# A decoder layer on one core: single projection groups, scores inside the projection, and four smaller moves of norms, picks and stores

## What is computed

```python
def mix_sample(x, win_k, win_v, sb_k_pool, sb_v_pool, mem_k, mem_v, page_table, mw):
    ...
    qa, ka, va, qb, kb, vb, qm = project_heads(rms_norm(x, g_pre), w_in)
    qa, ka = rope(qa, pos), rope(ka, pos)
    ...
    o_a = combine_by_denominators([dilated_group_gather(qa, k_all, v_all, n_buf, w, d) for w, d in DIL_PATTERNS])
    k_past = sb_k_pool[page_table].reshape(B, n_past, N_HEADS_SB, HEAD_DIM)
    ...
    o_b = sweep_query_blocks(lambda q, qp: stick_breaking_block(q, kb_all, vb_all, qp, sb_bias), qb, pos)
    o_m = memory_attention(qm, mem_k, mem_v)
    y = mixer_output(x, o_a, o_b, o_m, g_out_a, g_out_b, g_out_m, w_out, g_post)
```

## Time and profile before

| | us |
|---|---|
| three runs, median (lowest to highest) | 2225.07 (2220.13 to 2225.96) |
| the profiled execution, its own time | 2226.81 |
| span of its trace | 2225.0 |
| PE busy | 2137.6 (96%) |
| DVE, ACT, POOL busy | 1328.9, 925.1, 414.8 |
| mean granted TensorE clock | 0.986 of full speed |

### The profile page before, as it was taken

The page is one execution under the profiler, slowest core; times in us unless marked ns, Lnnn a source line. Parts: engine busy times, 40 slices in busy tenths (PEclk is TensorE's granted clock), DMA queues, the critical chain, the costliest instruction groups (busy, mean ns, idle before and its releaser), DMA issues.

```text
span 2225.0 us, 41421 instructions
## 1 busy us (share of the span) xinstructions
PE 2137.6 (96%) x16828; PEld 2039.5 (92%) x16828; DVE 1328.9 (60%) x3206; ACT 925.1 (42%) x1187; POOL 414.8 (19%) x349
## 2 busy tenths in 40 slices
PE   8999999999999999999959879899999999999999
PEld 8999999999999999999943339799999999999998
DVE  7555555555555686768694436675555555555555
ACT  4544443444343455334323414454434344343445
POOL 6100000000000043577611101440000000000001
PEclk9999999999999999999989989999999999999999
DMA  8455555555555456999999975355555555555552
GB/s 292 170 184 174 186 171 185 175 183 177 185 175 188 172 171 223 331 357 338 325 301 333 312 210 171 134 178 182 181 180 173 188 185 175 187 174 189 173 174 92
DMA packets 221889, 459.27 MB, mean 206 GB/s; under 512 B 11601, under 2 KB 12754, under 8 KB 220930
## 3 DMA queue, kind: packets, MB, share of 16 engines
q1 hardware_dynamic: 220226, 452.32, 60.0%
q0 software_dynamic: 1472, 4.29, 0.5%
HBM read 447.95 MB, written 8.62 MB: 205 GB/s over the span
## 4 chain that ended last, share of the span: by engine, by line
PE 51%; DMA 4%; DVE 3%; SPq 1%; issue 0%; ACT 0%; POOL 0%; DVEq 0%; POOLq 0%; ACTq 0%
PE ps L518 16%; PE ps L519 16%; PE ps L520 16%; DMA v_cache<-win_v 2%; DVE k_cache L1515 1%; PE ps L823 1%; DMA v_cache<-sb_v 1%; PE ps L698 1%; DMA late_values<-sb_v 1%; DVE head_space L1515 1%; PE ps L796 0%; SPq L443 0%; POOL acc L1824 0%; SPq L442 0%; PE ps L764 0%
## 5 line engine op out<-in xcount | busy, mean ns | idle before, releaser
L1304 DVE TENSOR_TENSOR wl<-raw,wh 128x1024 fp32r<-128x1024 f32 x592 | 732.5, 1242 | 698.8 <-ACT wh L931 698.1
L931 ACT ACTIVATE wh<-raw 128x1024 fp32r<-128x1024 f32 x656 | 691.7, 1059 | 1013.7 <-PE ps L520 990.8
L518 PE MATMUL ps<-xh,wh 128*128 128x264 f32 (+1 forms) x3776 | 1079.7, 286 | 19.4 <-DVE xl L1316 11.1
L519 PE MATMUL ps<-xl,wh 128*128 128x264 f32 (+1 forms) x3776 | 1077.3, 285 | 0.0
L520 PE MATMUL ps<-xh,wl 128*128 128x264 f32 (+1 forms) x3776 | 1076.7, 285 | 0.0
L518 PEld LDWEIGHTS ps<-xh,wh 128*128 128x128 f32 x3776 | 716.5, 190 | 22.3 <-issue 10.8
L519 PEld LDWEIGHTS ps<-xl,wh 128*128 128x128 f32 x3776 | 715.1, 189 | 0.2
L520 PEld LDWEIGHTS ps<-xh,wl 128*128 128x128 f32 x3776 | 713.5, 189 | 0.0
L520 PE MATMUL ps<-hh,wl 128*128 128x264 f32 x1408 | 400.2, 284 | 0.0
L518 PE MATMUL ps<-hh,wh 128*128 128x264 f32 x1408 | 400.2, 284 | 0.0
L519 PE MATMUL ps<-hl,wh 128*128 128x264 f32 x1408 | 400.1, 284 | 0.0
(11 more groups left out here) (259 smaller groups left out, 1111.1 us busy)
## 6 DMA issues: line engine op xcount, KB each, us to landing
raw<-w_gu SPq DMA_DIRECT2D x176, 1024.0 KB, 4.9
raw<-w_down SPq DMA_DIRECT2D x88, 1024.0 KB, 5.0
raw<-w_in SPq DMA_DIRECT2D x40, 1024.0 KB, 7.7
v_cache<-sb_v SPq DMA_DIRECT2D x90, 256.0 KB
k_cache<-sb_k SPq DMA_DIRECT2D x84, 256.0 KB
raw<-w_out SPq DMA_DIRECT2D x16, 1024.0 KB, 5.3
head_space<-sb_k SPq DMA_DIRECT2D x44, 256.0 KB
late_values<-sb_v SPq DMA_DIRECT2D x38, 256.0 KB
```

The source lines that it names most:

```text
L518: pe.matmul(out, w_hi, rh(k0 + kk), start=first and kk == 0, stop=False)
L519: pe.matmul(out, w_hi, rl(k0 + kk), start=False, stop=False)
L931: act.activation(wh[:, c % UNIT_SLOTS], raw_unit(c), ACT.Copy).then_inc(hi_made, 1)
L1304: dve.tensor_tensor(wl[:, c % UNIT_SLOTS], raw_unit(c), wh[:, c % UNIT_SLOTS].bitcast(F32), ALU.subtract).then_inc(lo_made, 1)
```

## The change

The first two projection groups are no longer interleaved: all ten run one after the other over six banks. Spreads 0 to 21 are put between units of the groups (`SPREAD_AT`), so that scores start in group 1; DVE takes nine tiles between two groups (`TAKE_AT`), 81 in all before the last take. Thirteen key tiles are loaded ahead, seven of them into memory that is free until later (`key_place`), from the fifth memory chunk on; from chunk 8 on SP puts two or three key tiles behind each weight chunk. ACT makes the squares of the mix norm earlier, and POOL adds them among its updates. The values are shared out over 18 parts instead of 17, so that eleven tiles are left behind the last head; among them PE sums the squares of the prompt's tokens and picks the paged heads, and DVE inverts the roots. For the eight samples a narrow sum, root and reciprocal follow. POOL stores six blocks of new values behind the last value tile instead of at once. The last four squares of `postm` are summed by PE.

```diff
 TURNED_GROUPS = (2, 3, 5, 6)
-ADD_AT = (11, 13, 19, 21, 35, 37, 43, 45)
+ADD_AT = (22, 24, 31, 33, 49, 51, 58, 60)
+TAKE_AT = (9, 18, 27, 36, 45, 54, 63, 72, 80)
+SPREAD_AT = {0: (1, 1), 1: (1, 2), 2: (2, 2), 3: (3, 1), 4: (4, 0), 5: (4, 6), 6: (5, 5), 7: (6, 4), 8: (7, 4),
+             9: (8, 0), 10: (8, 1), 11: (8, 2), 12: (8, 3), 13: (8, 4), 14: (8, 5), 15: (8, 6), 16: (8, 7), 17: (9, 0),
+             18: (9, 2), 19: (9, 2), 20: (9, 5), 21: (9, 5)}
+INSIDE = len(SPREAD_AT)
...
@@ -101,9 +128,13 @@
     return [sum_of(t)] if t >= 0 and value_tile(t)[1] in (PAGES // 2 - 1, MEM_TILE) else []
 
 
+REST = range(TILES * HEADS // (HEADS + 2), TILES)
+PICK_AT, ROOTS_AT = TILES - 3, REST[4]
+
+
 def share(i, part):
 
-    first, last = TILES * i // (HEADS + 1), TILES * (i + 1) // (HEADS + 1)
+    first, last = TILES * i // (HEADS + 2), TILES * (i + 1) // (HEADS + 2)
     at = (first, first + 2, first + 4, last)
     return range(at[part], at[part + 1])
 
...
@@ -454,30 +507,36 @@
             def load_keys(t):
 
                 b, k = key_tile(t)
-                if t >= K_SLOTS:
-                    sp.wait_ge(k_used, t - K_SLOTS + 1)
-                load_tile(b, k, key_slot(t), k_loaded[t % K_SLOTS], sb_k, win_k, mem_k)
-
-            for n in range(10):
+                if t >= FIRST_KEYS:
+                    sp.wait_ge(k_used, key_user(t) + 1)
+                load_tile(b, k, key_slot(t), key_loaded(t), sb_k, win_k, mem_k)
+
+            for n in range(8):
+                load_pair(CH_MEM + n, n, w_mem_kv[0], slice(0, 2))
+                if n == 4:
+                    sp.wait_ge(const_loaded, 16 * 10)
+                    sp.wait_ge(xl_ready["mem"], KT)
+                if n >= 4:
+                    load_keys(n - 4)
+            sp.wait_ge(unit_used, unit_of(CH_MEM))
+            for n in range(6):
                 load_in(n)
-            sp.wait_ge(const_loaded, 16 * 10)
-            sp.wait_ge(xl_ready["mem"], KT)
-            for t in range(2):
-                load_keys(t)
+                if n < 5:
+                    load_keys(n + 4)
             sp.wait_ge(squared["mix"], KT)
             sp.wait_ge(xl_ready["mix"], KT)
             sp.dma_start(x_park, xT[:].rearrange("p k t -> p (k t)")).then_inc(x_parked, 16)
-            for n in range(10, 12):
+            load_in(6)
+            sp.wait_ge(x_parked, 16)
+            for t in range(9, FIRST_KEYS):
+                load_keys(t)
+            load_in(7)
+            t = FIRST_KEYS
+            for n in range(8, 44):
                 load_in(n)
-            sp.wait_ge(x_parked, 16)
-            for t in range(2, K_SLOTS):
-                load_keys(t)
-            t = K_SLOTS
-            for n in range(12, 44):
-                load_in(n)
-                load_keys(t)
-                load_keys(t + 1)
-                t += 2
+                for _ in range(3 if n % 4 == 3 else 2):
+                    load_keys(t)
+                    t += 1
             for t in range(t, TILES):
                 load_keys(t)
 
...
@@ -675,8 +734,25 @@
             def in_group(g):
 
                 def free(j):
-                    pe.wait_ge(in_read, max(8, 4 * g + j - 5))
-                group(g * 8 + u_in, TOK, [block_bank(g, j) for j in range(4)], in_done, free)
+                    if g == 0:
+                        pe.wait_ge(memk_read, j + 1)
+                    elif g == 1 and j < 2:
+                        pe.wait_ge(memv_read, j + 1)
+                    else:
+                        pe.wait_ge(in_read, 4 * g + j - 5)
+
+                def spread_inside(c):
+                    if g == 0:
+                        pe.wait_ge(xl_ready["mix"], 2 * c + 2)
+                    if (g, c) == (0, 1):
+                        turn_memory_keys()
+                    if (g, c) == (0, 5):
+                        pe.wait_ge(mem_rows_made, 2)
+                        sum_partitions("mix", 6)
+                    for f, at in SPREAD_AT.items():
+                        if at == (g, c):
+                            spread(f)
+                group(g * 8 + u_in, TOK, [block_bank(g, j) for j in range(4)], in_done, free, spread_inside)
 
             def spread(f):
 
@@ -686,9 +762,9 @@
                     b, head, bank, before = f - 8, H_WIN + H_SB, 6 + f % 2, 8 * (f - 1) if f < 10 else 55 + f
                 else:
                     b, a = divmod(f - 16, 2)
-                    head, bank = 4 * a, (6 if b % 2 == 0 else 2) + a
-                    before = 71 + a if b == 0 else 72 + 3 * (b - 1) if b >= 2 else 0
-                pe.wait_ge(in_read, 8 if f < 8 else 20 if f < 16 else 40)
+                    head, bank = 4 * a, window_bank(b, a)
+                    before = (71 + a, 75, 78, 0)[b] if b < 4 else 72 + 3 * (b - 1)
+                pe.wait_ge(in_read, 4 if f < 8 else 20 if f < INSIDE else 40)
                 if f >= 16:
                     pe.wait_ge(roped, 4)
                 if before > 0:
@@ -699,24 +775,14 @@
                                    stop=True)
                 mm.then_inc(q_spread, 1)
 
...
-                    pe.wait_ge(memv_read, j + 1)
-                else:
-                    pe.wait_ge(mem_rows_made, j - 1)
-
-            two_groups(u_in, TOK, (0, 4), (in_done, in_done), (lambda j: pe.wait_ge(memk_read, j + 1), values_read),
-                       xl_ready["mix"], lambda: sum_beside("mix"), turn_memory_keys)
-            spread(0)
-            spread(1)
-            for g in range(2, 10):
+            for g in range(10):
                 in_group(g)
-                spread(g)
 
             pe.wait_ge(roped, 8)
             pe.wait_ge(in_read, 40)
             for f in range(10, 32):
-                spread(f)
+                if f >= INSIDE:
+                    spread(f)
                 r = f - 10
                 if r < 18:
                     if r >= 2:
...
@@ -848,25 +916,34 @@
                 for t in share(i, 2):
                     weigh_values(t)
                 turn(i)
-            for t in range(TILES * HEADS // (HEADS + 1), TILES):
+            for t in REST:
                 weigh_values(t)
-                if t == TILES - 3:
+                if t == REST[1]:
                     weigh(HEADS - 1)
-            pick_sums()
+                if t == ROOTS_AT:
+                    for i, name in enumerate(("out_a", "out_b", "out_m")):
+                        sum_partitions(name, i, a=i, width=SEQ)
+                if t == PICK_AT:
+                    pick_sums(True)
+            pick_sums(False)
 
 
             pe.wait_ge(sample_sq, 3)
-            for i, name in enumerate(("out_a", "out_b", "out_m")):
-                sum_partitions(name, i, a=i)
+            pe.matmul(ps[3][:, 0:3 * DEC], ones[:], acc[:, :, SEQ:TOK], start=True, stop=True).then_inc(sample_summed, 1)
             u_out = unit_of(CH_OUT)
             two_groups(u_out, TOK, (4, 0), (out_done, out_done),
-                       (lambda j: wait_one(j, o_read, HEADS), lambda j: wait_one(j, rooted, nth("out_m"))),
+                       (lambda j: wait_one(j, o_read, HEADS), lambda j: wait_one(j, sample_rooted, 3)),
                        xl_ready["out"], lambda: None)
             for g in range(2, 4):
                 group(u_out + 8 * g, TOK, 4 * ((g + 1) % 2), out_done,
                       lambda j: pe.wait_ge(out_read, 4 * (g - 2) + j + 1))
-            pe.wait_ge(out_read, 16)
-            sum_partitions("postm", 0)
+            pe.wait_ge(out_read, 12)
+            pe.wait_ge(squared["postm"], KT - 4)
+            pe.matmul(ps[4][:, 0:TOK], ones[:], acc[:, 0], start=True, stop=False)
+            for n in range(4):
+                pe.wait_ge(sq_made["postm"], KT - 4 + n + 1)
+                mm = pe.matmul(ps[4][:, 0:TOK], ones[:], out_sq[:, n], start=False, stop=n == 3)
+            mm.then_inc(summed, 1)
 
             ffn(1, CH_FFN2, "ffn2", lambda j: wait_one(j, rooted, nth("postm")), lambda j: None, lambda: None)
 
...
@@ -1117,18 +1195,19 @@
                 if c >= 4:
                     mix_upper(c - 4)
                 split(u_mem + 2 * c + 1 + AHEAD)
+                if c >= 4:
+                    for k in range(4 * c - 16, 4 * c - 12):
+                        square("mix", k, xT, x_ready["mix"], k + 1)
             for c in range(8):
-                split(u_in + 2 * c + AHEAD)
-                if c == 0:
+                split(u_in + c + AHEAD)
+                if c == 1:
                     for t in range(2):
                         act.wait_ge(memk_turned, t + 1)
                         act.activation(mem_out[:, t], ps[6 + t][:], ACT.Copy).then_inc(mem_rows_made, 1)
-                mix_upper(c + 4)
                 if c < 4:
-                    squares_behind("mix", 2 * c + 1)
-                    squares_behind("mix", 2 * c + 2)
-                split(u_in + 2 * c + 1 + AHEAD)
-            root_beside("mix", "post1")
+                    mix_upper(c + 4)
+                if c == 5:
```

(46 more changed lines are left out.)

87 lines of the change are left out of this document (58 added, 29 removed).

## The result

The changed kernel takes 2266.0 us (median; 2255.5 to 2273.3) against 2225.5 for the kernel before: a ratio of 1.0175, interval 1.0152 to 1.0198. The prediction was 2241, with a range of 2214 to 2258: slower, as forecast, but 25 us more than forecast and outside the range. The profiled execution is the slowest, 2273.3 (span 2271.5), 46.5 above the profiled one of before. The sums here are made on these two.

The account below looks back on a forecast made before the run. Bounds: PE in the projection, DVE in the key-tile tail, DMA for values, then PE. Terms 1.8 + 8.1 + 24.3 - 11.5 - 4.5 - 2.4 = +15.8 on 2226.81 gave 2242.6, median 2241; range 2214 to 2258.

Parts of the forecast that it names:

- Late weights: Projection: weight loads queued on SP behind key loads that wait for the running group's tiles make PE stall; +24.3 us.
- the term for the clock: Projection: three PE gaps over 2.50 us each cost 1.7 us through partly halved clock; 5.1 us in all.
- Start: Start of the projection: ACT's mix squares wait for POOL's adds, delaying splits and the memory-key copy; +1.8 us, bounds 0 and 4.
- End to first value load: Projection's end to first value load: fewer key tiles left, but DVE stands at tile 81; -11.5 us, 40.9 against 52.4.
- Behind the values: After the value tiles: early picks, narrow sum and root, smaller reciprocal, earlier last-head weighing; -4.5 us, bounds -2.5 and -6.
- picks and weighing: Behind the values: a quarter of the picks goes early, -0.9 us; last head's weighing ahead of the last tiles, -1.0.
- postm: At postm: four accumulating PE matmuls replace POOL's last four adds; -2.4 us, bounds 0 and -2.9.
- PE's work: In the projection: units, 22 spreads inside and small waits take 258.6 us instead of 250.45; +8.1 us.
- the six stores: Late stores moved behind the values, under an output projection with DMA to spare: no gain; 5 us cost if uncovered.
- the values as bound by bytes: Value stage: same bytes at the same full DMA, 159.7 us, so a change of 0.
- Rival 4: Projection: weights land in 7.9 us with half clock at each stall, 50 us; total 2266; chance 0.10 together with another rival.
- Rival 1: Projection: weight loads arrive in time, so the late-weights term is zero; sum -8.5 us, 2217; chance 0.20.

Follow-up runs that it names:

- e1: Changed kernel with every w_in and w_out load from chunk 9 on issued one chunk earlier on SP; 2225.1 us, ratio 0.9997.
- e3: Changed kernel with ACT's swap_halves put ahead of the late unit's split instead of behind it, in four places; 2254.5 us, ratio 1.0134.
- e2: Changed kernel with ACT's and POOL's splits of w_out's first three units moved behind the row copies and stores; 2256.8 us, ratio 1.0149.
- e4: Changed kernel with ACT's mix squares moved into the projection's first eight units, POOL's adds behind its updates, sum and root two units later; 2262.2 us, ratio 1.0155.
- e7: Kernel before the change with only those parts of the change that lie behind the projection; 2224.0 us, ratio 0.9986.
- e8: Changed kernel with earlier weight loads, four early spreads, later DVE chain and eight mix squares moved, plus unread PE matmuls near the values' end; 2223.0 us, ratio 0.9991.

## Why the prediction was off

*Late weights (+24.3, measured +30.0): mechanism right, the clock mis-sized.* The third chunk's load behind key 16 and its like, the waits of PE at unit 4 of groups 2, 3, 6 and 9 and at unit 0 of 4, 5, 7 and 8, the swap that doubles them: all were there, e1 takes them away and e3 some half of them. At these eight places PE waited 19.3 us, where 19.2 were forecast; four waits that I had not named, the longest of 1.3 at unit 4 of group 5, bring 21.2. The landings were longer than my 5.7 us (5.8 to 8.7 on the chain), but PE came to the late units later too, so its waits did not grow. What was too small is the term for the clock, 5.1: PE's busy time in the projection is 8.8 us longer than in e1 (266.6 and 257.7). And 30.0 is that of the slowest execution; by the same subtraction e2 has 25.2. The section of the Trainium skill that the prediction cites here (DMA: Bandwidth & Descriptors, "Anatomy of one DMA") states its fit for transfers that GpSimd issues. SP issues these, and the lone one of the earlier trace rows took 4.9 us.

*Start (+1.8, measured +6.6): wrong step.* I followed ACT through POOL's adds and gave DVE its times of the earlier trace rows unchanged. ACT was never what DVE waited for. POOL's sixteen adds beside DVE's own stream lengthened that stream by 6.3 us, and e4, without them, has the start back. My upper bound of 4 thought of POOL as the one that suffers.

*End to first value load (-11.5, measured -4.2): a queue forgotten.* DVE's stand at tile 81, softplus, chain and tiles came within a microsecond once the copies begin on time, as in e2. But I moved the key loads in SP's order and followed only w_in behind them; w_out's first two chunks stand in the same queue, and ACT splits three of their units ahead of the row copies. 7.4 us by e1, 8.1 by e2.

*Behind the values (-4.5, measured +2.0): picks and weighing mis-sized, and the clock left out.* From PE's last sum of squares to the output projection, 6.2 us before became 3.8 in the changed kernel and in e1 to e7: the narrow sum, root and reciprocal brought 2.3 of their 2.6. From tile 92 to that sum, 10.4 us before became 9.8 (e2) to 14.7 (the changed kernel), where I had taken off 1.9 for picks and weighing: in e7 the early picks take 1.06 us in the place where the last head's weighing had taken 1.13. The whole stretch is 13.6 to 15.7 in e1 to e7, so in those profiles the term is worth 1 to 3. The rest is the clock, which I left out. Two windows of the profiled execution of the changed kernel, to the first matmul of the output projection:

```profile
1353.00:1360.00 7.00, 6.75 (x24) 2.32 (x22) 2.25 (x3) 0.00 (x0) 0.00 (x0) 0.52 0.07 22
1360.00:1371.42 11.42, 5.91 (x26) 5.70 (x26) 4.69 (x17) 2.42 (x8) 3.40 (x6) 0.50 0.77 283
```

It ran this whole stretch at 1.2 GHz. PE had waited 1.3 and 1.8 us before its last two awaited tiles; that these waits are the cause is argued, not shown (e8 raised the clock with much more work). From tile 92 the same code has 0.68 in e1 and 0.82 in e2. This, and 3.3 us lost behind postm (granted clock 0.81 in the last 18.3 us, before 0.93 in the last 15.8), would make up the 7.3 by which this execution lies above the median; of the others there is no profile to show it. With -2 and 0 for these two, as the profiles of e1 to e7 have them, the misses sum to 23 of the 25 us by which 2241 fell short: start 4.8, work 0.5, late weights 5.7, end to first load 7.3, values 2.1, behind them 2.5, postm 0.5.

*Right:* PE's work (258.6 forecast, 259.1 in e1), postm (-1.9 for -2.4), the six stores at no visible cost (the output projection takes 96.5 us with and without them), and the values as bound by bytes, though with a spread of 10 us between profiles that I took as none.

*Rivals.* Rival 4 named 2266, but by 50 us of late weights, of which there were 30; so the time came out by luck, through the terms that it held unchanged. Rival 1 is what e1 makes of the kernel: 2217 forecast, 2225 measured, 5 us of the rest the late start (854.12).

## What to carry to other kernels

When loads of one kind move within an in-order issue queue, follow every other load behind them to its user, past the end of the stage too: one chunk of lead was worth 41 us here, as much as the whole change had lost. An engine that shows no idle time can still be lengthened by what runs beside it: compare mean durations, not only waits. And a first transfer can be pulled forward only until the next wait in its own queue decides.

## What the runs showed of the hardware

Beside POOL adds, DVE's operations on two SBUF tiles of 128x264 averaged 0.94 and 0.98 us instead of 0.65 and 0.79, with no wait shown anywhere; single ones took 0.48 to 0.49 us with no POOL work beside them and 0.97 to 1.00 with POOL work throughout. Loads of 1 MB among key loads landed in 5.6 to 11.2 us (median 8.0), in e1, where they no longer held anything up, in 5.9 to 11.9 (median 8.5). And the same code from tile 92 to the output projection took between 13.6 us at a mean granted clock of 0.82 (e2) and 18.6 us at 0.51 (the changed kernel); what brought the clock down there is not shown.
